# Second layer of a four-layer kernel: seven half-size products in another order, VectorE's weight sums moved, one weight quarter and the squares in places of their own

## What is computed

```python
u = modulated_norm(x)                                # 512 latent + 256 context tokens, width 1024
q, k, v, z = split(u @ w_in, 4)                      # 4 x 2048 columns; k, v also for the context
q = rms_norm(q per head of 64, qn_g); k = rms_norm(k per head of 64, kn_g)
s = q @ band(k) * scale + bias, masked;  s_ctx = q @ k_ctx * scale
p = softmax(concat(s, s_ctx))                        # per head, in fp32
out = (p_band @ band(v) + p_ctx @ v_ctx) * silu(z)   # gate
x = x + gate_row * (out @ w_out)
```

## Time and profile before

| | us |
|---|---|
| median of three runs | 3306.05 (3302.7 to 3309.83) |
| the profiled execution | 3304.96 |
| its span in the trace | 3303.1 |
| second layer's projections, first matmul to the last turn with one | 1257 to 2015 |
| turn 0, 16, 32 begin on PE | 1380.18, 1581.21, 1780.83 |

### The profile page before, as it was taken

One profiled execution on the slowest core, in us unless ns is written; L12 is line 12 of the kernel. 1 busy time (PEld: TensorE's weight loads), 2 busy tenths in 40 slices (PEclk: granted clock), 3 DMA queues, 4 the chain that ended last, 5 costly groups with the idle time before them and its releaser, 6 DMA issues. The chain is left out here.

```text
span 3303.1 us, 38110 instructions
## 1 busy us (share of the span) xinstructions
PE 3053.1 (92%) x14382; PEld 1977.1 (60%) x14382; DVE 1549.1 (47%) x3530; ACT 834.9 (25%) x2300; POOL 492.6 (15%) x785
## 2 busy tenths in 40 slices
PE   5999999999999997999999999968999999589699
PEld 2445555555555546777778776547888886244374
DVE  2245455455454336555565554433455564331431
ACT  1013333333333212133232332311212221120131
POOL 1122232132130102212020210000011110110000
PEclk8999999999999998999999999978999999799899
DMA  6420110110121004111212023041211100311001
GB/s 230 170 85 26 34 44 26 43 34 26 51 83 70 1 32 132 59 45 46 58 52 77 26 73 139 1 113 26 52 26 26 52 26 1 108 53 65 26 1 51
DMA packets 138461, 189.21 MB, mean 57 GB/s; under 512 B 22268, under 2 KB 91036, under 8 KB 136228
## 3 DMA queue, kind: packets, MB, share of 16 engines
q1 hardware_dynamic: 137080, 186.70, 17.7%
q10 hardware_dynamic: 1200, 0.09, 0.0%
HBM read 177.10 MB, written 9.67 MB: 57 GB/s over the span
## 5 line engine op out<-in xcount | busy, mean ns | idle before, releaser
L488 PE MATMUL a_psP<-a_w,a_uT 128*128 128x512 f32 x1536 | 700.5, 601 | 7.2 <-DMA a_w<-a_w_in 7.2
L488 PEld LDWEIGHTS a_psP<-a_w,a_uT 128*128 128x128 f32 x1536 | 280.6, 192 | 324.8 <-issue 324.8
L737 DVE TENSOR_REDUCE a_small<-a_psS 128x1 f32<-128x768 f32 (+1 forms) x192 | 140.7, 774 | 402.0 <-PE a_psS L516 402.0
L2236 PE MATMUL d_ps<-d_uT,d_w 128*128 128x264 f32 x1024 | 243.1, 391 | 13.9 <-DVE d_yT L2597 8.6
L2236 PEld LDWEIGHTS d_ps<-d_uT,d_w 128*128 128x128 f32 x1024 | 191.6, 192 | 49.1 <-DVE d_yT L2597 10.6
L1441 PE MATMUL b_psP<-b_w,b_uT 128*128 128x256 f32 x768 | 188.4, 390 | 0.8 <-issue 0.8
L643 ACT ACTIVATE a_e<-a_psS,a_small 128x768 f32<-128x768 f32 (+1 forms) x192 | 143.8, 753 | 139.1 <-DVE a_small L737 138.7
L1441 PEld LDWEIGHTS b_psP<-b_w,b_uT 128*128 128x128 f32 x768 | 145.3, 194 | 26.3 <-issue 7.9
L1759 DVE TENSOR_REDUCE b_small<-b_psS 128x2 f32<-128x512 f32 x64 | 44.2, 690 | 227.0 <-PE b_psS L1494 227.0
L538 PEld LDWEIGHTS a_psO<-a_v,a_pT 128*128 128x128 f32 x896 | 115.1, 192 | 45.9 <-issue 45.9
L650 ACT COPY a_pT<-a_psS 128x768 f32<-128x768 f32 (+1 forms) x96 | 63.0, 656 | 311.4 <-PE a_psS L525 311.4
(11 more groups left out here) (466 smaller groups left out, 5430.2 us busy)
## 6 DMA issues: line engine op xcount, KB each, us to landing
a_w<-a_w_in SPq DMA_DIRECT2D x16, 2048.0 KB, 8.6
b_w<-b_w_in SPq DMA_DIRECT2D x64, 512.0 KB, 4.1
d_w<-a_w_in SPq DMA_DIRECT2D x32, 512.0 KB, 7.2
a_yT<-mod_w SPq DMA_DIRECT2D x8, 1536.0 KB, 8.4
a_yT<-mod_w SPq DMA_DIRECT2D x8, 1024.0 KB, 17.0
b_bias<-bias_table SPq DMA_DIRECT2D x64, 128.0 KB
a_yT<-mod_w SPq DMA_DIRECT2D x8, 512.0 KB, 7.6
a_w<-a_w_out SPq DMA_DIRECT2D x2, 2048.0 KB, 7.8
```

The lines of the kernel that those rows point to most:

```text
L488: ins = nc.tensor.matmul(s.psP[:, x % 2, :], s.uT[:, a, t * P:(t + 1) * P], w[:, a, :], start=(a == 0), stop=(a == KD - 1))
L737: nc.vector.tensor_reduce(self.nm[i % 2][:, k:k + 1], self.score_banks(k, keys), AX_X, ALU.max, negate=True).then_inc(self.mx, 1)
L2236: ins = nc.tensor.matmul(ps[:, 4, 0:n], s.w[:, h % 2, b, i, :], s.uT[:, b, half * n:(half + 1) * n], start=(b == 0), stop=(b == KD - 1))
```

## The change

The order of products becomes 1, 2, 6, 5, 3, 7, 4, and the adds follow it. T1 and T2 of the next chunk stand behind the adds of products 3 and 4 of the last step, T3 and T4 behind those of products 2 and 6 of the first step. A sum that would fall among the early adds is held and made at the head of the late ones, except T2, which is made where it stands, with what is held. The quarter b12 is loaded into tiles 12 and 13 of `yT`, as soon as T3 of the chunk before is made; T3 is written to the b12 quarter of `w` as before. ACT's squares alternate between `sq` and tile 14 of `yT`, so a square waits for the use of the one two before. For z tiles DVE's use of the tanh moves from before `weights` to after it. The norm's dump moves to `raw`. The waits in `project` are as they were.

```diff
-        self.dump = flat[:, NT * D:(NT + 1) * D]
+        self.dump = s.raw[:, 2:4, :].rearrange("p a n -> p (a n)")
...
+        self.squares = [self.sq[:, :], self.yT[:, 14, :]]
+        self.b12 = self.yT[:, 12:14, :].rearrange("p a n -> p (a n)").rearrange("p (a n) -> p a n", a=4)
...
-    ORDER = (1, 2, 6, 3, 7, 4, 5)
-    READ = (1, 2, 3, 4, 5, 6, 8)
+    ORDER = (1, 2, 6, 5, 3, 7, 4)
+    READ = (1, 2, 3, 4, 5, 7, 8)
...
     def load(self, sp, b, n):
         g, k = divmod(b, 4)
-        if b:
+        if b and n < 3:
             before = g * self.N + sum(x[2] for x in self.kinds[:k])
-            sp.wait_ge(self.done, 7 * (before - 1) + (1, 2, 4, 5)[n])
+            sp.wait_ge(self.done, 7 * (before - 1) + (1, 2, 5)[n])
+        elif b:
+            sp.wait_ge(self.ts, 4 * (b - 1) + 3)
...
             g, k = divmod(b, 4)
+            self.load(sp, b, 3)
...
-            for n in range(4):
+            for n in range(3):
...
             act.wait_ge(self.parts, 8 * (x + 1))
-            self.free(act, f)
+            if f >= 2:
+                self.used(act, f - 2)
...
-            nc.scalar.activation(s.sq[:, :], src, fn, scale=scale).then_inc(self.sq, 1)
+            nc.scalar.activation(s.squares[f % 2], src, fn, scale=scale).then_inc(self.sq, 1)
...
+        t3 = s.w[:, 0:4, self.H:]
...
-            ins = nc.vector.tensor_tensor(b12, b22, b12, ALU.subtract)
+            ins = nc.vector.tensor_tensor(t3, b22, b12, ALU.subtract)
...
-        if p == 5 and self.chunk(x)[2] and self.chunk(x)[0] + 1 < 4 * NG:
-            for i in (1, 2):
-                self.weight_sum(dve, self.chunk(x)[0] + 1, i)
...
+        elif p == 5:
+            dve.wait_ge(self.parts, n + 3)
+            nc.vector.tensor_tensor(c22, part, ps, ALU.add).then_inc(self.parts, 1)
         elif p == 3:
-            dve.wait_ge(self.parts, n + 3)
-            nc.vector.tensor_tensor(c12, part, ps, ALU.add).then_inc(self.parts, 1)
+            dve.wait_ge(self.parts, n + 4)
+            nc.vector.tensor_tensor(c12, c22, ps, ALU.add).then_inc(self.parts, 1)
         elif p == 7:
-            nc.vector.tensor_tensor(c22, part, ps, ALU.add).then_inc(self.parts, 1)
...
+            nc.vector.tensor_tensor(c22, c22, ps, ALU.add).then_inc(self.parts, 1)
+            nc.vector.tensor_tensor(c21, part, ps, ALU.add).then_inc(self.parts, 1)
         else:
...
+            dve.wait_ge(self.parts, n + 7)
+            nc.vector.tensor_tensor(c21, c21, ps, ALU.subtract).then_inc(self.parts, 1)
+
+    def add_parts(self, dve, i, early):
...
+        if not early:
+            for b, n in self.held:
+                self.weight_sum(dve, b, n)
+            self.held = []
+        for j in (self.early if early else self.late)[i]:
+            self.add_part(dve, j)
+            p = self.ORDER[j % 7]
+            b, first, last = self.chunk(j // 7)
+            n = 0
+            if last and b + 1 < 4 * NG and p in (3, 4):
+                b, n = b + 1, {3: 1, 4: 2}[p]
+            elif first and p in (2, 6):
+                n = {2: 3, 6: 4}[p]
+            if n == 2 or (n and not early):
+                for held in self.held:
+                    self.weight_sum(dve, *held)
+                self.held = []
+                self.weight_sum(dve, b, n)
+            elif n:
+                self.held.append((b, n))
...
             for tile in self.finish[i]:
-                use_squares(*tile)
+                sum_squares(*tile)
```

More of the change, by code:

```diff
@@ L1333, in out_weights, with quarter @@
         return tiles[:, e - first, :], i
-    def blocks(self, n):
+    def quarter(self, n):
         a, c = ((0, 0), (4, 0), (4, 1), (0, 1))[n]
-        return slice(a, a + 4), slice(self.H * c, self.H * (c + 1))
+        return a, c, (self.s.b12 if n == 3 else self.s.w[:, a:a + 4, self.H * c:self.H * (c + 1)])
     def load(self, sp, b, n):
         g, k = divmod(b, 4)
-        if b:
+        if b and n < 3:
             before = g * self.N + sum(x[2] for x in self.kinds[:k])
-            sp.wait_ge(self.done, 7 * (before - 1) + (1, 2, 4, 5)[n])
[L1347 to L1350, removed]
+            sp.wait_ge(self.done, 7 * (before - 1) + (1, 2, 5)[n])
+        elif b:
+            sp.wait_ge(self.ts, 4 * (b - 1) + 3)
+        a, c, home = self.quarter(n)
+        c0 = (g + self.kinds[k][1] * NG) * GROUP + self.H * c
+        sp.dma_start(home, self.w_in[a * P:(a + 4) * P, c0:c0 + self.H].rearrange("(a p) n -> p a n", p=P)
+                     ).then_inc(self.w_in_sem[n], 16)
     def sync(self, sp):
@@ L1613, in scalar, with used @@
                 copy_weights(i)
[L1615 to L1632, removed]
+    def used(self, eng, f):
+        kinds = [tile[1] for i in sorted(self.finish) for tile in self.finish[i]][:f + 1]
+        if kinds[f] == "z":
+            eng.wait_ge(self.zdone, kinds.count("z"))
+        else:
+            eng.wait_ge(self.red, len(kinds) - kinds.count("z"))
     def gpsimd(self, pool):
@@ L1677, in weight_sum @@
         nc, s = self.nc, self.s
-        b11, b21, b22, b12 = (s.w[:, rows, cols] for rows, cols in (self.blocks(i) for i in range(4)))
+        b11, b21, b22, b12 = (self.quarter(i)[2] for i in range(4))
         t1, t2, t4 = (s.wt[:, i, :, :] for i in range(3))
+        t3 = s.w[:, 0:4, self.H:]
         if n == 1:
@@ L1720, in add_part @@
         dve.wait_ge(self.done, j + 1)
-        if kind in "kq" and p in (2, 7):
-            before = self.heads_index(g, kind, 2 * pr + (p == 7)) - 4
+        if kind in "kq" and p in (2, 5):
+            before = self.heads_index(g, kind, 2 * pr + (p == 5)) - 4
             if before >= 0:
                 dve.wait_ge(self.tp, before + 1)
-        if p == 5 and self.chunk(x)[2] and self.chunk(x)[0] + 1 < 4 * NG:
-            for i in (1, 2):
-                self.weight_sum(dve, self.chunk(x)[0] + 1, i)
         if p == 1:
@@ L1737, in add_part @@
             nc.vector.tensor_tensor(part, part, ps, ALU.add).then_inc(self.parts, 1)
+        elif p == 5:
+            dve.wait_ge(self.parts, n + 3)
+            nc.vector.tensor_tensor(c22, part, ps, ALU.add).then_inc(self.parts, 1)
         elif p == 3:
-            dve.wait_ge(self.parts, n + 3)
-            nc.vector.tensor_tensor(c12, part, ps, ALU.add).then_inc(self.parts, 1)
+            dve.wait_ge(self.parts, n + 4)
+            nc.vector.tensor_tensor(c12, c22, ps, ALU.add).then_inc(self.parts, 1)
         elif p == 7:
-            nc.vector.tensor_tensor(c22, part, ps, ALU.add).then_inc(self.parts, 1)
-        elif p == 4:
-            dve.wait_ge(self.parts, n + 5)
-            nc.vector.tensor_tensor(c21, c22, ps, ALU.subtract).then_inc(self.parts, 1)
-        else:
[L1747 to L1750, removed]
+            nc.vector.tensor_tensor(c22, c22, ps, ALU.add).then_inc(self.parts, 1)
+            nc.vector.tensor_tensor(c21, part, ps, ALU.add).then_inc(self.parts, 1)
+        else:
+            dve.wait_ge(self.parts, n + 7)
[21 more added lines that the diff above has]
+                self.held.append((b, n))
     def vector(self, dve):
@@ L1792, in gate, with sum_squares @@
             nc.vector.tensor_tensor(s.yT[:, g * 4 + p, cols], s.psO[:, 0:P], s.z[:, p, cols], ALU.mult).then_inc(self.gy, 1)
-        def use_squares(g, kind, t, f):
-            dve.wait_ge(self.sq, f + 1)
+        def sum_squares(g, kind, t, f):
             if kind == "z":
-                z = s.z[:, t, :]
-                nc.vector.scalar_tensor_tensor(z, s.sq[:, :], 1.0, z, ALU.add, ALU.mult).then_inc(self.zdone, 1)
                 return
             j = self.heads_index(g, kind, t)
-            nc.vector.reduce_sum(self.ss[:, j % 2, :], s.sq[:, :].rearrange(view, h=HG), AX_X).then_inc(self.red, 1)
+            dve.wait_ge(self.sq, f + 1)
+            nc.vector.reduce_sum(self.ss[:, j % 2, :], s.squares[f % 2].rearrange(view, h=HG), AX_X).then_inc(self.red, 1)
         def evacuate(g, kind, t, f):
             if kind == "z":
+                dve.wait_ge(self.sq, f + 1)
+                z = s.z[:, t, :]
+                nc.vector.scalar_tensor_tensor(z, s.squares[f % 2], 1.0, z, ALU.add, ALU.mult).then_inc(self.zdone, 1)
                 return
@@ L1840, in vector @@
                 maxima(i)
-            for j in self.early[i]:
-                self.add_part(dve, j)
+            self.add_parts(dve, i, True)
             if lead in (1, 2):
@@ L1854, in vector @@
                 gate(i - 1)
-            for j in self.late[i]:
-                self.add_part(dve, j)
+            self.add_parts(dve, i, False)
             for q in self.out_ended(i - 1):
```

## The result

The changed kernel takes 3318.15 us, the median of eight runs (3313.55 to 3322.53). The kernel before, run beside it, takes 3305.81 us (eight runs, 3301.6 to 3310.63). The ratio is 1.0034 [1.0024, 1.0044]: slower by 12.3 us, clear of the 0.2% that can be told from no change. The profiled execution took 3319.45 us, with a span of 3317.6.

The account below looks back on a forecast made before the run. PE, busy 92% of the span, bounds the kernel, so gains come from its waits or clock. Losses 36.9 minus gains 30.7 give +6.2 us on a median of 3306.05: forecast 3312 us, range 3300 to 3323.

Parts of the forecast that it names:

- the fourth rival: Low clock lasts 6 us after several new waits, or gains of turns 4 to 11 vanish: 3318 to 3326, chance 0.25.
- the forecast itself: The prediction's own band around 3312 us, 3305 to 3317, chance 0.53.
- The double buffer and turn 2: PE's waits before the softmax transposes go: 0.6 us won in turns 4 and 6 each, 9.3 in three turns like 2.
- Turns 10 and 11: `gate` bounds both turns in each group: 2.3 us won of 4.4 together, without clock.
- the z chunks: At the first product 6 of each z chunk only T2 stands ahead, not T1 + T2: 3.1 us won of 3.9.
- The clock given back: Low clock behind the waits of turn 11 and one of turn 2 goes with those waits: 7.8 us come back.
- T4 in turn 8: PE waits for held T4 behind second evacuation and `gate`: 4.9 us lost, three times, 14.7, without clock.
- T4 in the lead: Held T4 makes PE wait: turns -9 and -5 lose 8.2 us together, turn -15 loses 4.2, without clock.
- Two new waits for T2: For turn -9 it put PE's arrival 1.0 us later, T2 being a little late behind T1 and three adds.
- T4 and the port: DVE's second evacuation waits out POOL's gain, 1.74 us; T4 takes 1.2 us if first, some 2.2 if the gain is.
- the clock behind the waits: PE's clock drops to 0.50 behind each of six T4 waits of 5 to 7 us: 1.6 us each, 9.8 together.

Follow-up runs that it names:

- experiment 3: The kernel before with only the second buffer for the squares added; order of products, sums and tanh use stay: 3281.8 us, ratio 0.993.
- Experiment 1: The changed kernel with T4 made directly behind the add of product 6, also when that add is an early one: 3275.82 us, ratio 0.9913.
- Experiment 7: The changed kernel, T4 still held, with DVE's `gate` ahead of the evacuations in turns that finish k or q tiles: 3302.23 us, ratio 0.9991.
- experiment 2: The kernel before with only T4 moved behind the add of product 6 and held to the late adds: 3346.77 us, ratio 1.0122.
- experiment 4: The changed kernel with T4 made at once and POOL's first gain waiting for both evacuations, lead included: 3272.55 us, ratio 0.9898.

## Why the forecast held, and where it was off

The forecast of 3312 us was 6 us low. 3318.15 us is inside the range of 3300 to 3323, but it falls in the band of the fourth rival, "more is lost" (3318 to 3326), that had 0.25, and above that of the forecast itself (3305 to 3317). Of that rival's two reasons the first came true in part (a low clock that lasts), the second did not (the gains of turns 4 to 11 are there). Step by step:

- **The double buffer and turn 2**: right. The gain in turns 4 and 6 is 0.58 and 0.66 where 0.6 was worked out, because `gate` behind POOL's chain takes the other half: waits of 0.81 and 0.5 us stand where they were put. Turns 10 and 11 fit as well. The sum of all gains (30.7 forecast, 31.3 measured) is closer than its parts: with the clock, turn 2 and its like gave 0.7 us more than forecast, turns 10 and 11 gave 0.8 less and the z chunks 0.6 more, and these nearly cancel. The split between the causes was less good: experiment 3 shows 23 us for the buffer alone, where its expectation gave 12 to 19.
- **The clock given back**: right, 1.00 behind turn 11 and turn 2. Experiment 1 bears the sum out: 30.7 of gain without losses gave 3275, measured were 3275.82. That it fits so closely is in part luck, since there turns 8, 24 and 40 are 0.3 us longer than before, not shorter, and the lead is 1.1 us longer.
- **T4 in turn 8**: right in mechanism and place, low in size. Two terms are off. T4 beside the gain was taken as the middle of 1.2 and 2.2 us, 4.9 us a turn; the gain was first in all three (waits of 6.72, 6.71 and 6.71, less the old 1.21: 5.5 each). That is 1.8 us in all. The clock behind the wait was taken as 1.6 us. From the first matmul behind T4 to the next scores the turns take 8.84, 6.47 and 6.75 us, the kernel before 6.23 - 1.21 = 5.02 for the same work: 3.8, 1.4 and 1.7 us lost to the clock. So it fits in two groups and is more than twice that in the first, where 0.50 holds for over 6 us. Some 0.16 us a turn beside that I have not placed.
- **T4 in the lead**: right in place; turn -5 came out as forecast, turns -9 and -15 lost 1.0 and 1.2 us more. There 1.6 of clock was too little: the eight records of the waiting product alone lose 3.75 - 1.89 = 1.9, and 0.50 goes on for 5 us behind turn -15. Counted from the first matmul behind T4 over the same work, the clock costs 2.8 us in turn -15, 2.6 in turn -9 and 1.6 in turn -5, which is the whole difference.
- **Two new waits for T2** of 0.84 and 0.85 us stand in turns -10 and -6, where the kernel before has none. They cost nothing of their own, as forecast for turn -9: PE gets to T4 later by as much and T4 waits on DVE, not on PE.
- **T4 and the port.** It was argued that the second evacuation waits out the gain, and that it would be so in the groups too. It was, with 1.74 us in turn 8 as in turn -9 before. The Trainium skill (SBUF — State Buffer, Who interferes with whom) has the rule that VectorE with two SBUF inputs and GpSimd reading SBUF lock each other out for the whole instruction, and that the order of issue decides who blocks. Experiment 7 shows both orders of one pair, so the trace agrees. In each order the first keeps its own length (1.26, 1.21) and the second takes nearly what is left of the first and its own length: 1.22 + 1.22 = 2.44 us against 2.30 measured for T4, 1.05 + 1.26 = 2.31 against 2.18 for the gain. In neither order are both stretched.

So the step that was off is the loss by T4, 43.4 us by the turns and 36.9 in the forecast. Of the 6.5 us between them the port has 1.8, the clock in turn 8 and its like 2.1 (6.9 against 3 x 1.6), the lead 2.2, and 0.5 are not placed (rounding makes up the rest). So the mechanism held, and the term that was too small is the clock behind the waits: 1.6 us each, where it cost 1.4 to 3.8. The cause itself is shown from both sides: taking the hold away gives 42 us back, adding it alone to the kernel before takes 42.

What stays open is why the clock fell behind some waits and not behind others of the same length, even in one kernel. Experiment 3 has three such waits of 2.2 us. In the kernel before, the waits of turns 2 and 18 (3.18 and 3.07 us) left the clock at 1.00, but behind that of turn 34 (3.09 us) it was 0.63 over 3 us. The prediction read the first of these alone in its rows and counted the third among the losses of the clock. This was seen, not caused at will.

## What to carry to other kernels

A step that is moved on an engine that works in order has to be costed by what stands between its old and its new place, not by its own length: T4 is 1.22 us, and putting it behind evacuations that wait for POOL (in turn -15 behind those of the norm) made PE wait 5 to 7 us each time, though DVE is idle half of the time. Where a step waits for another engine, put whatever PE needs ahead of it and let the waiting step be last (`gate` ahead of the evacuations: 16 us for one moved call). And look at the parts of a mixed change one by one: here 29 us of gain and 42 us of loss came out as 12 us slower.

## What the runs showed of the hardware

- A VectorE sum over 1024 columns with both inputs in SBUF took 1.22 us alone and 2.30 when a gain of 1.26 us had started 0.04 us before it. When it started first, it took 1.21 and the gain 2.18. A lead of 0.04 us was enough to decide which of the two pays.
- TensorE's clock fell to 0.50 behind every long wait for T4, of 4.9 to 7.3 us: six in the changed kernel, six in experiment 2. Waits of 2.2 us split: all four in the lead of experiment 4 were followed by 0.50, the three in turn 11 and its like of experiment 3 by 1.00, 0.51 and 0.72. The waits of 3.18 and 3.07 in the kernel before kept 1.00, those of 3.09 and 3.34 didn't.
- How long the low level lasts differs too: over 6 us behind the 6.72 us wait of turn 8, while its like in the next two groups, with waits of 6.71 us and the same work behind them, lost only 1.4 and 1.7 us in place of 3.8.
